# A long convolution split into even and odd positions: half-size transforms, sums and differences, columns dealt out anew

## Chip, cores and metric

One NeuronCore of one Trainium2 chip runs the whole program. The metric is device time of one execution in microseconds (us). TensorE is called PE, its weight loads PEld, VectorE DVE, ScalarE ACT, GpSimd POOL and SyncE SP.

## The reference

The program is three layers on 256 tokens of width 2048, batch 1, float32: a gated recurrent mixer, a forgetting-attention mixer, and a block with two branches and a feed-forward part. The change is in the first branch of that block, a Hyena mixer of width 1024:

```python
def two_sided_spectrum(h):
    kern = jnp.concatenate([h_fwd, jnp.zeros_like(h_fwd[:1]), h_bwd[:0:-1]], axis=0)
    return jnp.fft.rfft(kern, axis=0)

def long_conv(u, kf, bias):
    uf = jnp.fft.rfft(u, n=2 * L, axis=1)
    y = jnp.fft.irfft(uf * kf[None], n=2 * L, axis=1)[:, :L]
    return y + u * bias
...
    z = hx1 * long_conv(hv, kf[:, 0], hb[0])
    y_a = (hx2 * long_conv(z, kf[:, 1], hb[1])).astype(x.dtype)
...
    mixed = gate_a * (y_a @ w_branch_a[l]) + gate_b * (y_b @ w_branch_b[l])
```

L is 256. So there are two long convolutions one after the other over 1024 channels, each with its own filters, and then the product `y_a @ w_branch_a`. The product `y_b @ w_branch_b` of the other branch does not depend on them.

## The kernel before

**Matrix products.** Weights come as a stream of chunks of 512 KB (128x1024 floats) through a ring of four buffers. For each chunk ACT writes a rounded part `hi` and DVE the rest `lo` (`prep`, L539 and L1046; in loops `chunk`, L534 and L1040), and PE runs three passes for each tile (L1853 to L1855). SP starts the load of a ring slot as soon as `lo` of its old chunk is written. The product `y_b @ w_branch_b` (called br_b) is done in 16 *columns*, one chunk and 24 PE instructions each (`branch_column`): PE computes column f into PSUM bank f % 2, and DVE multiplies it by its gate (`filled`, L1738, counted in the semaphore `branch_b`). PE may not start column f before `branch_b` has reached f - 1. `ahead(f)` prepares the chunk that is four columns further on.

**The long convolution** is laid between those columns. It works in four *units* u: units 0 and 1 are the first and second convolution of channels 0 to 511, units 2 and 3 those of channels 512 to 1023, so unit 1 needs the output of unit 0 and unit 3 that of unit 2. Transforms are float32 matmuls with constant cosine and sine matrices (`dftm`, 256x256 each for forward and inverse). A float32 matmul is two instructions in the records (two passes). For each unit:

- `y_filters` (PE, L2280): the filters of 512 channels in time; `windowed` (DVE): times a window, then the sum (`y_SUM`) and the difference (`y_FB`) of forward and backward filter;
- `y_filter_cosines`, `y_filter_sines` (PE, L2267, 4 matmuls of 128x512 each): filter spectra, which ACT copies to `y_K` (L937);
- `y_turn` (PE, L2298, 8 transposes of 128x128), `turned` (ACT, L931): the input with positions on partitions (`y_U`);
- `y_input_spectrum` (PE, L2267 `y_T,dftm`): 4 cosine and 4 sine matmuls of 128x512 into banks 2, 3 and 6, 7;
- `spectra_product` (DVE, L1706 to L1713): six operations of 128x1024; in unit 3 twelve of 128x512;
- `y_back` (PE, L2337): 16 matmuls of 128x256, the inverse transform straight back to channels on partitions;
- `gated` (DVE, L1722 and L1729): adds the bias term and multiplies by the gate, which `y_turn` of the next unit waits for (`y_out`).

All orders are written out by hand, per engine. `columns_mid` and `columns_end` say which columns stand between the input spectrum and `y_back`, and which after it. After the last column comes `product(prod["br_a"])`, the product with `w_branch_a`; its input is the convolution's output, in pieces 2 and 3 (`branch_piece`: ACT rounds into `XH`, L518, DVE writes the rest into `XL`, L1111). `own_last` and `own_wait` make DVE wait for its own results.

Of the kernel before, what the change touches and what calls it, by code (L numbers as in the profile page):

```python
# [180 lines left out]
def program(nc, stream, h_in, params, consts, masks_a, mask_fox, mask_ml, dft, windows, z_pos, w1, w2, w3, out):  # L181
# [13 lines left out]
    with ExitStack() as ctx:  # L195
# [112 lines left out]
        with ExitStack() as ph:  # L308
# [9 lines left out]
            with ExitStack() as sub:  # L318
                w3_t = sb(sub, "w3_t", [FILT, 4, 512])
                y_win = sb(sub, "y_win", [P, 2, 2, 512])  # L320
                y_T = [sb(sub, f"y_T{s}", [P, 2, 512]) for s in range(2)]
                y_SUM = sb(sub, "y_SUM", [P, 2, 512])
                MR = sb(sub, "MR", [MH, 2, 4, SEQ])

            y_U = y_T[0]
# [186 lines left out]
        def _(act):  # L512
# [377 lines left out]
            def mixers():  # L890
# [38 lines left out]
                def turned(u):  # L929
                    act.wait_ge(S("y_ut"), u + 1)  # L930
                    act.activation(y_U[:, :, :], PS[:, 2:4, :], ACT.Copy).then_inc(S("y_u"), 1)  # L931
# [34 lines left out]
                ahead(columns_mid[3])  # L966
                act.wait_ge(S("y_out"), 4)
                branch_piece(3)
                ahead(columns_end[3])
# [47 lines left out]
        def _(dve):  # L1017
# [656 lines left out]
            def hyena():  # L1674
# [18 lines left out]
                def spectra_product(u):  # L1693
                    dve.wait_ge(S("y_uspec"), u + 1)
                    dve.wait_ge(S("y_k"), 2 * u + 2)
                    if u:
                        dve.wait_ge(S("y_inv"), u)

                    n_parts = 2 if u == 3 else 1
                    for part in range(n_parts):  # L1700
                        w = 512 // n_parts
                        cols = slice(w * part, w * part + w)
                        uc, us = PS[:, 2:4, cols], PS[:, 6:8, cols]
                        t0, t1 = (y_T[i][:, :, cols] for i in range(2))
                        k0, k1 = (y_K[:, i, :, cols] for i in range(2))
                        own_last(dve.tensor_tensor(t0, uc, k0, ALU.mult))  # L1706
                        own_last(dve.tensor_tensor(t1, us, k1, ALU.mult))
                        own_wait()
                        own(dve.tensor_tensor(t0, t0, t1, ALU.subtract), "y_spectrum", 2 * (u + part) + 1)
                        own_last(dve.tensor_tensor(t1, uc, k1, ALU.mult))  # L1710
                        own_last(dve.tensor_tensor(k0, us, k0, ALU.mult))
                        own_wait()
                        own(dve.tensor_tensor(t1, t1, k0, ALU.add), "y_spectrum", 2 * (u + part) + 2)  # L1713
                    dve.sem_inc(S("y_prod"), 1)

                def gated(u):

                    half, o = u // 2, u % 2
                    dve.wait_ge(S("y_inv"), u + 1)
                    for j in range(4):  # L1720
                        t = 4 * half + j
                        own_last(dve.scalar_tensor_tensor(out=HY[:, t, :], in0=HY[:, t, :],  # L1722
                                                          scalar=pc("hyena_bias", HT * o + t),
                                                          in1=PS[:, y_back_bank[u] + j // 2,
                                                                 SEQ * (j % 2):SEQ * (j % 2) + SEQ],
# [30 lines left out]
                columns((1,))  # L1756
                for u in range(4):
                    spectra_product(u)
                    if u == 3:
                        branch_piece(2)  # L1760
                    columns(columns_mid[u])
                    gated(u)
                    if u < 2:
                        windowed(u + 2)
                    if u == 3:
                        filled(14)
                        branch_piece(3)
                        ahead(14)
                        columns((15,))
                    else:  # L1770
                        columns(columns_end[u])
# [78 lines left out]
        def _(pe):  # L1850
# [420 lines left out]
            def y_filters(u):  # L2271
# [5 lines left out]
                for b in range(4):  # L2277
                    if u == 0 and b == 2:
                        pe.wait_ge(S("m_fw"), 2 * MH)
                    pe.matmul(PS[:, filter_bank[u][b], :], h2T[:, 128 * (b % 2):128 * (b % 2) + 128],  # L2280
# [11 lines left out]
            def y_turn(u):  # L2292
# [3 lines left out]
                for k in range(2):  # L2296
                    for j in range(4):
                        ins = pe.transpose(PS[:, 2 + k, 128 * j:128 * j + 128],  # L2298
                                           HY[:, 4 * (u // 2) + j, 128 * k:128 * k + 128], ident)
                ins.then_inc(S("y_ut"), 1)  # L2300

            def y_input_spectrum(u):
                pe.wait_ge(S("y_u"), u + 1)
                y_spectrum(2, cos_f, y_U)
# [4 lines left out]
                y_spectrum(6, sin_f, y_U).then_inc(S("y_uspec"), 1)  # L2309
# [16 lines left out]
            def y_back(u):  # L2326

                pe.wait_ge(S("y_spectrum"), 2 * u + 2)
                if u == 3:
                    pe.wait_ge(S("y_k"), 2 * u + 2)  # L2330
                for j in range(4):
                    if u == 3 and j == 2:
                        pe.wait_ge(S("y_spectrum"), 2 * u + 4)
                    n = 0
                    for part, m in enumerate((cos_i, sin_i)):
                        for f in range(2):
# [157 lines left out]
```

## Time and profile before

| | us |
|---|---|
| median of 3 runs | 2662.69 (2659.71 to 2662.83) |
| the profiled execution: its own time / its span | 2660.54 / 2658.5 |
| PE busy | 2609.9 (98%), 21346 instructions |
| DVE busy | 1567.9 (59%) |
| ACT busy | 1202.1 (45%) |
| mean granted PE clock | 0.996 |
| convolution phase (first filter spectrum to the start of br_a) | 1636.45 to 1787.87 |

The busy time of a group is the union of its instructions. A matmul's duration in the records is longer than the distance to the next, since matmuls overlap, so costs are read from start to start.

### The profile page before, as it was taken

To read this page: it belongs to the slowest core of one execution; us is meant where nothing else is said; L and a number is where in the kernel's file an instruction comes from. 1 tells how busy PE (TensorE), PEld (TensorE's weight loads), DVE (VectorE), ACT (ScalarE), POOL (GpSimd) and SP (SyncE) were. 2 spreads that over 40 slices of the span, in tenths; PEclk is the share of its full clock that TensorE was granted. 3 is DMA by queue.
4 is the path that set the end of the run, shared out by engine and by line. 5 is a ranking of instruction groups with operands and counts; after the bars stand their busy time and mean duration, and the time that the engine had idled before them with its cause. 6 is when DMAs were issued, how large, how long until landed. Compare 5 with 4: busy or idle time off the path is not lost.

```text
span 2658.5 us, 53149 instructions
## 1 busy us (share of the span) xinstructions
PE 2609.9 (98%) x21346; PEld 2537.8 (95%) x21346; DVE 1567.9 (59%) x1934; ACT 1202.1 (45%) x1404; POOL 44.2 (2%) x48
## 2 busy tenths in 40 slices
PE   8999999999999999999999999999999999999997
PEld 8999999999999999999999996679999999999997
DVE  6445777564465666677755456556565555554544
ACT  5344466543357655533435443124444444444442
POOL 0000121000000000000000000000000000000000
PEclk9999999999999999999999999999999999999999
DMA  6554532455544434555555553115555656565553
GB/s 225 175 178 163 171 104 76 167 174 183 174 174 153 139 114 149 193 196 190 192 193 185 193 194 104 48 65 193 188 193 185 202 184 200 188 198 192 189 198 128
DMA packets 123705, 446.05 MB, mean 168 GB/s; under 512 B 13594, under 2 KB 15925, under 8 KB 123440
## 3 DMA queue, kind: packets, MB, share of 16 engines
q1 hardware_dynamic: 122208, 438.82, 49.2%
q0 software_dynamic: 1360, 5.27, 0.6%
q8 instruction: 102, 1.67, 0.3%
q14 instruction: 35, 0.29, 0.0%
HBM read 441.94 MB, written 2.10 MB: 167 GB/s over the span
## 4 chain that ended last, share of the span: by engine, by line
PE 91%; DVE 4%; ACT 2%; issue 2%; DMA 0%; POOL 0%; DVEq 0%; SPq 0%; ACTq 0%
PE PS L1853 25%; PE PS L1855 25%; PE PS L1854 25%; PE PS L1916 2%; PE PS L1918 2%; PE PS L1917 2%; PE PS L2267 2%; PE PS L2337 1%; DVE lo L1046 1%; PE PS L2219 1%; ACT hi L539 0%; PE PS L2000 0%; PE PS L2016 0%; PE PS L2280 0%; PE PS L2099 0%
## 5 line engine op out<-in xcount | busy, mean ns | idle before, releaser
L1853 PE MATMUL PS<-XH,hi 128*128 128x256 f32 (+1 forms) x5152 | 1449.9, 281 | 21.6 <-DVE lo L1040 11.2
L1855 PE MATMUL PS<-XH,lo 128*128 128x256 f32 (+1 forms) x5152 | 1446.1, 281 | 0.0
L1854 PE MATMUL PS<-XL,hi 128*128 128x256 f32 (+1 forms) x5152 | 1441.5, 280 | 0.0
L1040 DVE TENSOR_TENSOR lo<-raw,hi 128x1024 fp32r<-128x1024 f32 x704 | 852.8, 1224 | 752.9 <-ACT hi L534 749.6
L534 ACT ACTIVATE hi<-raw 128x1024 fp32r<-128x1024 f32 x704 | 740.3, 1059 | 946.4 <-PE PS L1855 920.9
L1853 PEld LDWEIGHTS PS<-XH,hi 128*128 128x128 f32 x5152 | 970.7, 188 | 26.7 <-issue 18.8
L1854 PEld LDWEIGHTS PS<-XL,hi 128*128 128x128 f32 x5152 | 973.3, 189 | 1.4 <-issue 1.2
L1855 PEld LDWEIGHTS PS<-XH,lo 128*128 128x128 f32 x5152 | 970.6, 188 | 0.0
L1916 PE MATMUL PS<-XH,hi 128*128 128x256 f32 (+1 forms) x768 | 229.3, 299 | 0.3 <-DVE XL L1111 0.3
L1918 PE MATMUL PS<-XH,lo 128*128 128x256 f32 (+1 forms) x768 | 216.1, 281 | 0.0
L1917 PE MATMUL PS<-XL,hi 128*128 128x256 f32 (+1 forms) x768 | 215.9, 281 | 0.0
L1046 DVE TENSOR_TENSOR lo<-raw,hi 128x1024 fp32r<-128x1024 f32 x124 | 152.2, 1232 | 106.2 <-ACT hi L539 105.8
L1853 PE MATMUL PS<-GH,hi 128*128 128x256 f32 x704 | 194.4, 276 | 0.0
L1854 PE MATMUL PS<-GL,hi 128*128 128x256 f32 x704 | 194.4, 276 | 0.0
L1855 PE MATMUL PS<-GH,lo 128*128 128x256 f32 x704 | 194.4, 276 | 0.0
L539 ACT ACTIVATE hi<-raw 128x1024 fp32r<-128x1024 f32 x124 | 129.3, 1050 | 96.5 <-PE PS L1855 63.2
L1916 PEld LDWEIGHTS PS<-XH,hi 128*128 128x128 f32 x768 | 144.7, 188 | 2.9 <-issue 1.4
L1917 PEld LDWEIGHTS PS<-XL,hi 128*128 128x128 f32 x768 | 144.7, 188 | 1.5
L1918 PEld LDWEIGHTS PS<-XH,lo 128*128 128x128 f32 x768 | 144.4, 188 | 0.0
L1855 PEld LDWEIGHTS PS<-GH,lo 128*128 128x128 f32 x704 | 132.1, 188 | 0.0
L1854 PEld LDWEIGHTS PS<-GL,hi 128*128 128x128 f32 x704 | 132.1, 188 | 0.0
L1853 PEld LDWEIGHTS PS<-GH,hi 128*128 128x128 f32 x704 | 132.1, 188 | 0.0
(322 smaller groups left out, 1570.2 us busy)
## 6 DMA issues: line engine op xcount, KB each, us to landing
raw<-stream SPq DMA_DIRECT2D x828, 512.0 KB, 4.0
H<-h_in SPq DMA_DIRECT2D x4, 544.0 KB, 7.8
y_win<-windows POOLq DMA_DIRECT2D x2, 1024.0 KB, 7.2
out<-H SPq DMA_DIRECT2D x4, 512.0 KB, 3.8
w_t<-w POOLq DMA_DIRECT2D x2, 512.0 KB, 6.3
dftm<-dft POOLq DMA_DIRECT2D x1, 1024.0 KB, 8.0
ml_m<-mask_ml POOLq DMA_DIRECT2D x1, 512.0 KB, 3.9
a_m<-masks_a POOLq DMA_DIRECT2D x1, 272.0 KB, 6.0
```

The source lines that it names most:

```text
L534: act.activation(halves(hi, s, q.tokens), raw_halves(s), ACT.Copy).then_inc(hi_ready, 1)
L539: act.activation(halves(hi, k % RING, tokens_of(k)), raw_halves(k % RING), ACT.Copy).then_inc(hi_ready, 1)
L1040: dve.tensor_tensor(halves(lo, s, q.tokens), raw_halves(s), halves(hi, s, q.tokens).bitcast(F32), ALU.subtract)\
L1046: dve.tensor_tensor(halves(lo, k % RING, tokens_of(k)), raw_halves(k % RING), halves(hi, k % RING, tokens_of(k)).bitcast(F32), ALU.subtrac ...
L1853: pe.matmul(PS[:, bank, 0:n], w_hi, x_hi, start=start, stop=False)
L1854: pe.matmul(PS[:, bank, 0:n], w_hi, x_lo, start=False, stop=False)
L1855: return pe.matmul(PS[:, bank, 0:n], w_lo, x_hi, start=False, stop=stop)
L1916: pe.matmul(dst, hi[s][:, col], x_hi, start=k == 0, stop=False)
L1917: pe.matmul(dst, hi[s][:, col], x_lo, start=False, stop=False)
L1918: ins = pe.matmul(dst, lo[s][:, col], x_hi, start=False, stop=k == NT - 1)
L2219: ins = pe.matmul(PS[:, 4 + 2 * d + tb, 0:2 * P + 1], w[:, st, 128 * tb:128 * tb + 128], m_VT[:, st, h, :], start=st == 0, stop=st == 1)
L2267: ins = pe.matmul(PS[:, bank + f, :], dftm[:, m, k, 128 * f:128 * f + 128], src[:, k, :], start=k == 0, stop=k == 1)
```

## The change

What it does, in four parts:

1. **Order of positions and frequencies.** The constant matrices and windows are laid out anew: positions in the order even, then odd; frequencies k = 0 to 127, then 255 down to 128. For frequency k and its mirror 255 - k the even positions give the same cosine half and the odd ones the same but for its sign, so one 128x128 matrix serves for both. The filter matmuls and the transposes read their weights with a step of two (`h2T[:, b % 2::2]`, `HY[..., k::2]`).
2. **Input spectrum.** `y_parities` transforms the even and the odd half only (4 matmuls of 128x512 instead of 8). ACT copies the two odd halves from PSUM (`odds`), and DVE forms sum and difference (`butterflies`).
3. **Product and inverse.** `spectra_product` runs in two parts of 256 channels with eight operations each, the last two of which form sum and difference over the mirrored frequencies; `y_back` too has two parts, and each of its 16 matmuls moves 128 columns instead of 256. `gated` reads its PSUM operand with the two position halves interleaved.
4. **Columns.** One column goes between the two parts of `y_back`; column 1 moves from before unit 0 into it. PE no longer waits for `y_out` before br_a.

```diff
-            columns_mid = ((2, 3), (5, 6), (8, 9), (11, 12, 13))
-            columns_end = ((4,), (7,), (10,), (14, 15))
+            columns_mid = ((1, 2), (5, 6), (9, 10), (13, 14))
+            columns_last = (3, 7, 11, 15)
+            columns_end = ((4,), (8,), (12,), ())
...
+                def odds(u):
+                    for i in range(2):
+                        act.wait_ge(S("y_odd_spec"), 2 * u + i + 1)
+                        if i == 0:
+                            act.wait_ge(S("y_sums"), 2 * min(u + 2, 4))
+                        act.activation(y_FB[:, 1, i, :], PS[:, 3 + 4 * i, :], ACT.Copy).then_inc(S("y_odd"), 1)
...
-                ahead((0, 1))
+                ahead((0,))
                 for u in range(3):
+                    odds(u)
+                    ahead(columns_mid[u])
+                    ahead((columns_last[u],))
                     spectrum(u + 1, 0)
-                    ahead(columns_mid[u])
                     spectrum(u + 1, 1)
                     turned(u + 1)
                     ahead(columns_end[u])
+                odds(3)
...
+                def butterflies(u):
+
+                    if u:
+                        dve.wait_ge(S("y_inv"), 2 * u)
+                    for i in range(2):
+                        dve.wait_ge(S("y_uspec"), 2 * u + i + 1)
+                        dve.wait_ge(S("y_odd"), 2 * u + i + 1)
+                        even, odd = PS[:, 2 + 4 * i, :], y_FB[:, 1, i, :]
+                        own_last(dve.tensor_tensor(y_T[:, 1 - i, 0, :], even, odd, ALU.add))
+                        own_last(dve.tensor_tensor(y_T[:, 1 - i, 1, :], even, odd, ALU.subtract))
+                    own_wait()
+
+                def spectra_product(u, part):
+
                     dve.wait_ge(S("y_k"), 2 * u + 2)
...
+                    own_last(dve.tensor_tensor(acc, x0, k1, ALU.mult))
+                    own_last(dve.tensor_tensor(x0, x0, k0, ALU.mult))
+                    own_last(dve.tensor_tensor(k0, x1, k0, ALU.mult))
+                    own_last(dve.tensor_tensor(k1, x1, k1, ALU.mult))
+                    own_wait()
+                    own_last(dve.tensor_tensor(x1, k0, acc, ALU.subtract))
+                    own_last(dve.tensor_tensor(x0, x0, k1, ALU.add))
+                    own_wait()
+                    low, high = y_T[:, :, 0, cols], y_T[:, :, 1, cols]
+                    dve.tensor_tensor(acc, low, high, ALU.add).then_inc(S("y_spectrum"), 1)
+                    dve.tensor_tensor(low, low, high, ALU.subtract).then_inc(S("y_spectrum"), 1)
...
+                        y = HY[:, t, :].rearrange("p (n a) -> p n a", a=2)
+                        conv_out = PS[:, y_back_bank[u] + j // 2, SEQ * (j % 2):SEQ * (j % 2) + SEQ]
+                        own_last(dve.scalar_tensor_tensor(out=y, in0=y, scalar=pc("hyena_bias", HT * o + t),
+                                                          in1=conv_out.rearrange("p (a n) -> p n a", a=2),
                                                           op0=ALU.mult, op1=ALU.add))
...
+                for u in range(3):
+                    first, second = columns_mid[u]
+                    butterflies(u)
+                    spectra_product(u, 0)
+                    filled(first)
+                    spectra_product(u, 1)
+                    filled(second)
+                    filled(columns_last[u])
+                    ahead(first)
                     gated(u)
+                    ahead(second)
+                    ahead(columns_last[u])
                     if u < 2:
                         windowed(u + 2)
...
+                butterflies(3)
+                filled(13)
+                spectra_product(3, 0)
+                filled(14)
+                spectra_product(3, 1)
+                branch_piece(2)
+                ahead(13)
+                filled(15)
+                gated(3)
+                ahead(14)
+                branch_piece(3)
+                ahead(15)
...
+            def y_parities(bank, m):
+
+                pe.matmul(PS[:, bank + 1, :], dftm[:, m, 1, 0:128], y_U[:, 1, :], start=True, stop=True)\
+                    .then_inc(S("y_odd_spec"), 1)
+                return pe.matmul(PS[:, bank, :], dftm[:, m, 0, 0:128], y_U[:, 0, :], start=True, stop=True)
...
-                y_back(u)
+                y_back(u, 0)
+                branch_column(columns_last[u])
+                y_back(u, 1)
...
-            pe.wait_ge(S("y_out"), 4)
             pe.wait_ge(S("branch_b"), NT)
             product(prod["br_a"])
```

The input spectrum of unit 0 and the filter spectrum behind it, on PE. Before:

```order
L2267 MATMUL PS<-y_T,dftm 128x512 [waits y_u]
L2267 MATMUL PS<-y_T,dftm 128x512 x3
L2267 MATMUL PS<-y_T,dftm 128x512 [waits y_windowed]
L2267 MATMUL PS<-y_T,dftm 128x512 x3
L2267 MATMUL PS<-y_SUM,dftm 128x512 [waits y_sums]
L2267 MATMUL PS<-y_SUM,dftm 128x512 x3
```

The same place on PE in the changed kernel, where it now follows directly on `y_filters(1)`, without column 1 between:

```order
L2312 MATMUL PS<-w_t,h2T 128x512 x3
L2336 MATMUL PS<-y_T,dftm 128x512 [waits y_u]
L2338 MATMUL PS<-y_T,dftm 128x512
L2336 MATMUL PS<-y_T,dftm 128x512 [waits y_windowed]
L2338 MATMUL PS<-y_T,dftm 128x512
L2299 MATMUL PS<-y_SUM,dftm 128x512 [waits y_sums]
L2299 MATMUL PS<-y_SUM,dftm 128x512 x3
```

Eight matmuls of the input spectrum became four; those of the filter spectrum are as many as before.

The inverse transform of unit 0 on PE, before:

```order
L2337 MATMUL PS<-dftm,y_T 128x256 [waits y_spectrum]
L2337 MATMUL PS<-dftm,y_T 128x256 x15
L2267 MATMUL PS<-y_FB,dftm 128x512 [waits y_sums]
L2267 MATMUL PS<-y_FB,dftm 128x512 x3
L2298 MATMUL PS<-cst,HY 128x128 [waits y_out]
L2298 MATMUL PS<-cst,HY 128x128 x7
```

And its first part in the changed kernel, with the start of column 3 behind it:

```order
L2374 MATMUL PS<-dftm,y_FB 128x128 [waits y_spectrum]
L2374 MATMUL PS<-dftm,y_FB 128x128
L2374 MATMUL PS<-dftm,y_T 128x128 x2
L2374 MATMUL PS<-dftm,y_FB 128x128 x2
L2374 MATMUL PS<-dftm,y_T 128x128 x2
L1885 MATMUL PS<-XH,hi 128x256 [waits lo_ready,branch_b]
```

The moved operand shrinks from 256 to 128 columns, and the second eight matmuls stand behind a column (24 instructions).

The product of unit 3 on DVE, before: the second half of it, and what follows.

```order
L1706 TENSOR_TENSOR y_T<-PS,y_K 128x2x256 [waits y_spectrum]
L1707 TENSOR_TENSOR y_T<-PS,y_K 128x2x256
L1709 TENSOR_TENSOR y_T<-y_T 128x2x256 [waits dve_own]
L1710 TENSOR_TENSOR y_T<-PS,y_K 128x2x256 [waits y_spectrum]
L1711 TENSOR_TENSOR y_K<-PS,y_K 128x2x256
L1713 TENSOR_TENSOR y_T<-y_T,y_K 128x2x256 [waits dve_own]
L1111 TENSOR_TENSOR XL<-HY,XH 128x1024 [waits y_spectrum,xh_ready]
L1738 TENSOR_TENSOR MG<-MG,PS 128x256 [waits chunk_used]
```

In the changed kernel, behind the butterflies of unit 3: `filled(13)`, the product's part 0, `filled(14)` and the start of part 1.

```order
L1759 TENSOR_TENSOR MG<-MG,PS 128x256 [waits chunk_used,dve_own]
L1723 TENSOR_TENSOR y_FB<-y_T,y_K 128x2x256 [waits y_k]
L1724 TENSOR_TENSOR y_T<-y_T,y_K 128x2x256
L1725 TENSOR_TENSOR y_K<-y_T,y_K 128x2x256
L1726 TENSOR_TENSOR y_K<-y_T,y_K 128x2x256
L1728 TENSOR_TENSOR y_T<-y_K,y_FB 128x2x256 [waits dve_own]
L1729 TENSOR_TENSOR y_T<-y_T,y_K 128x2x256
L1732 TENSOR_TENSOR y_FB<-y_T 128x2x256 [waits dve_own]
L1733 TENSOR_TENSOR y_T<-y_T 128x2x256
L1759 TENSOR_TENSOR MG<-MG,PS 128x256 [waits chunk_used]
L1723 TENSOR_TENSOR y_FB<-y_T,y_K 128x2x256 [waits y_k]
```

Six operations for each half became eight, four butterflies came ahead of them, and the first of the `filled` now stands ahead of the product and not behind it.

## Rows read from the trace of the kernel before

**Rows 1.** The page's first part: busy time and share of the span.

```profile
PE 2609.9 (98%) x21346; PEld 2537.8 (95%) x21346; DVE 1567.9 (59%) x1934; ACT 1202.1 (45%) x1404; POOL 44.2 (2%) x48
```

**Rows 2.** Timeline of PE, unit 0 to 1: start, duration, line, operation, count.

```profile
1653.59 7.03 PE L2267 MATMUL PS<-y_T,dftm 128*128 128x512 f32 x16
1660.45 3.60 PE L2267 MATMUL PS<-y_SUM,dftm 128*128 128x512 f32 x8
...
1669.41 7.07 PE L2337 MATMUL PS<-dftm,y_T 128*128 128x256 f32 x32
1676.31 3.60 PE L2267 MATMUL PS<-y_FB,dftm 128*128 128x512 f32 x8
```

**Rows 3.** Timeline of PE, the transposes of unit 0 and what follows them.

```profile
1639.95 1.04 PE L2298 MATMUL PS<-cst,HY 128*128 128x128 f32 x8
1640.83 3.60 PE L2267 MATMUL PS<-y_FB,dftm 128*128 128x512 f32 x8
```

**Rows 4.** Groups by line: small float32 matmuls of another layer, summed busy, mean ns.

```profile
L2016 PE MATMUL PS<-AB,a_SS 128*128 128x64 f32 x128 | 17.8, 262 | 0.0
L2000 PE MATMUL PS<-a_VT,a_KT 128*128 128x128 f32 x128 | 16.9, 275 | 0.0
```

**Rows 5.** Waits of PE from 1625 to 1800: us in total, times, longest.

```profile
PE PS L1853 <- DVE MG L1738: 4.4, 1, 4.4
PE PS L1853 <- issue: 1.3, 1, 1.3
```

**Rows 6.** Timeline of DVE, product of unit 3 to column 11's gate.

```profile
1758.35 0.69 DVE L1706 TENSOR_TENSOR y_T<-PS,y_K 128x512 f32<-128x512 f32 x1 [4.49 <-PE PS L2267]
1758.95 0.68 DVE L1707 TENSOR_TENSOR y_T<-PS,y_K 128x512 f32<-128x512 f32 x1
1759.67 0.69 DVE L1709 TENSOR_TENSOR y_T<-y_T 128x512 f32<-128x512 f32 x1
...
1765.82 0.69 DVE L1713 TENSOR_TENSOR y_T<-y_T,y_K 128x512 f32<-128x512 f32 x1
1766.66 1.23 DVE L1111 TENSOR_TENSOR XL<-HY,XH 128x1024 fp32r<-128x1024 f32 x1
1767.80 0.41 DVE L1738 TENSOR_TENSOR MG<-MG,PS 128x256 f32<-128x256 f32 x1
```

**Rows 7.** Timeline of PE: end of column 12, start of 13, inverse of unit 3.

```profile
1763.55 0.28 PE L1855 MATMUL PS<-XH,lo 128*128 128x256 f32 x1
1768.27 0.58 PE L1853 MATMUL PS<-XH,hi 128*128 128x256 f32 x1 [4.44 <-DVE MG L1738]
...
1773.55 1.61 PE L2337 MATMUL PS<-dftm,y_T 128*128 128x256 f32 x5
```

**Rows 8.** Stretches: us, PE busy (count), PEclk (1.00 is full), DMA share, GB/s.

```profile
1763.50:1767.00 3.50, 0.33 (x3) 1.00 0.00 0
1767.00:1767.50 0.50, 0.00 (x0) 0.96 0.00 0
1767.50:1774.00 6.50, 5.73 (x26) 0.50 0.45 149
1774.50:1787.00 12.50, 12.02 (x79) 1.00 0.13 43
```

**Rows 9.** Timeline of DVE, `gated` of unit 0 (its first row with the wait).

```profile
1676.51 1.66 DVE L1722 SCALAR_TENSOR_TENSOR HY<-HY,par,PS 128x256 f32<-128x256 f32 x4 [3.75 <-PE PS L2337]
1678.20 1.22 DVE L1729 TENSOR_TENSOR HY<-HY 128x1024 f32<-128x1024 f32 x1
```

**Rows 10.** Groups of ACT: copies out of PSUM, and an operation of 128x512.

```profile
L937 ACT ACTIVATE y_K<-PS 128x1024 f32<-128x1024 f32 x8 | 8.2, 1029 | 70.8 <-DVEq L1714 39.5 <-PE PS L2267 31.3
L810 ACT ACTIVATE b_PT<-PS 128x384 f32<-128x384 f32 x16 | 7.8, 486 | 22.7 <-PE PS L2114 22.7
```

**Rows 11.** Waits of SP's queue from 1625 to 1800: what its weight loads waited for.

```profile
SPq L452 <- DVE lo L1046: 172.9, 16, 43.0
```

**Rows 12.** Timeline of DVE, the gate of column 15, the last `filled`.

```profile
1787.35 0.42 DVE L1738 TENSOR_TENSOR MG<-MG,PS 128x256 f32<-128x256 f32 x1
```

More of the change, by code:

```diff
@@ L966, in mixers @@
                 ahead(columns_mid[3])
+                ahead((columns_last[3],))
                 act.wait_ge(S("y_out"), 4)
                 branch_piece(3)
[L969 removed]
             q = prod["br_b"]
@@ L1691, in windowed @@
                         .then_inc(S("y_sums"), 1)
-                def spectra_product(u):
-                    dve.wait_ge(S("y_uspec"), u + 1)
-                    dve.wait_ge(S("y_k"), 2 * u + 2)
[L1696 to L1714, printed above, removed]
@@ new lines, in spectra_product @@
+                def spectra_product(u, part):
+                    dve.wait_ge(S("y_k"), 2 * u + 2)
+                    cols = slice(SEQ * part, SEQ * part + SEQ)
+                    acc = y_FB[:, 1, :, cols]
+                    x0, x1 = (y_T[:, i, :, cols] for i in range(2))
+                    k0, k1 = (y_K[:, i, :, cols] for i in range(2))
+                    own_last(dve.tensor_tensor(acc, x0, k1, ALU.mult))
[9 more added lines that the diff above has]
+                    dve.tensor_tensor(low, low, high, ALU.subtract).then_inc(S("y_spectrum"), 1)
+                    if part:
+                        dve.sem_inc(S("y_prod"), 1)
@@ L1755, in hyena @@
                 windowed(1)
[L1756 to L1761, printed above, removed]
+                for u in range(3):
[7 more added lines that the diff above has]
+                    ahead(first)
                     gated(u)
+                    ahead(second)
+                    ahead(columns_last[u])
                     if u < 2:
                         windowed(u + 2)
[L1765 to L1771, printed above, removed]
+                    columns(columns_end[u])
+                butterflies(3)
[10 more added lines that the diff above has]
+                ahead(15)
             q = prod["mg"]
@@ L2324, in branch_column, with y_back @@
                 ins.then_inc(chunk_used, 1)
-            def y_back(u):
-                pe.wait_ge(S("y_spectrum"), 2 * u + 2)
+            def y_back(u, part):
+                pe.wait_ge(S("y_spectrum"), 2 * (2 * u + part) + 2)
                 if u == 3:
                     pe.wait_ge(S("y_k"), 2 * u + 2)
[L2331 to L2336, printed above, removed]
-                            ins = pe.matmul(PS[:, y_back_bank[u] + j // 2, SEQ * (j % 2):SEQ * (j % 2) + SEQ],
-                                            y_T[part][:, f, 128 * j:128 * j + 128], dftm[:, m, f, :],
-                                            start=n == 0, stop=n == 3)
-                            n += 1
+                for j in (2 * part, 2 * part + 1):
+                    for a in range(2):
+                        col = SEQ * (j % 2) + 128 * a
+                        for i, m in enumerate((sin_i, cos_i)):
+                            w = (y_T[:, i, 0, :] if a else y_FB[:, 1, i, :])[:, 128 * j:128 * j + 128]
+                            ins = pe.matmul(PS[:, y_back_bank[u] + part, col:col + 128], w,
+                                            dftm[:, m, 0, 128 * a:128 * a + 128], start=i == 0, stop=i == 1)
                 ins.then_inc(S("y_inv"), 1)
```

30 lines of the change are left out of this document (14 added, 16 removed).

## The prediction

> **What bounds the kernel now.** First the busy shares: PE is busy for 98% of the span [rows 1], so time is won by taking work or idle time from PE, and what DVE or ACT do counts only where PE waits for them. Then the timeline of PE through one unit. From 1653.59 to 1660.45 stand the 16 passes of the input spectrum, 6.86 us or 0.429 a pass; the filter spectrum behind it has 8 passes, so it ends at 1660.45 + 3.43 = 1663.88; two columns follow up to 1669.41, 2.76 each; and the 32 passes of the inverse run to 1676.31, 6.90 or 0.216 a pass [rows 2]. Nothing lies between them: in units 0 to 2 PE is the bound. Third, the waits of PE in the phase: 4.4 us for a gate `filled`, once, and 1.3 once [rows 5]. The timeline puts the first into unit 3: PE ends column 12 soon after 1763.55 and starts column 13 at 1768.27 [rows 7], because DVE does the twelve operations of the product in one go from 1758.35, then the piece of `XL`, and only then the gate of column 11 at 1767.80 [rows 6]. The second is the start of br_a, which wants the gate of column 15; it begins at 1787.35 and ends at 1787.77 [rows 12]. Last, the granted clock. It stood at 1.00 up to 1767.0, fell to 0.50 before 1767.5, some 3.7 us after the last matmul, was 0.50 up to 1774 and 1.00 again behind that [rows 8]: the lower of the two levels, 1.2 GHz instead of 2.4.
>
> **Work taken from PE.** The input spectrum goes from 16 passes of 512 columns to 8: 8 x 0.429 = 3.43 us a unit, 13.7 in four. The inverse keeps its 32 passes but moves 128 columns in each. The nearest row is the transposes, also float32, 128x128, new weights each time: 8 from 1639.95 to 1640.83, 0.110 each [rows 3]. So 32 x 0.110 = 3.5 for 6.9, 3.4 a unit, 13.5 in four. From below 64 columns take no less than half of that, yet 128 such passes come to 17.8 us (0.139), and 128 passes of 128 columns to 16.9 (0.132), gaps between their groups counted in [rows 4]: weight loads, not columns, might set the pace. At 0.132 the inverse would save 2.8 less; I take 0.110, from a run without gaps as here, and see no reason for less. Together **27.2 us**.
>
> **The clock.** Column 13 took 1773.55 - 1768.27 = 5.28 instead of 2.76, and the passes of the inverse up to 1774 lost 0.3: **2.9 us**, if the new kernel does not let the clock fall.
>
> **Work added on DVE and ACT, and whether it hides.** The steps: operations of 512 elements start 0.60 apart, 0.72 where one waits for the one before [rows 6]; DVE sees a result of PE 0.20 after its last pass (1676.31, 1676.51) [rows 2, 9], PE one of DVE about 0.1 after its end. A product part is eight operations with two such waits: 3 x 0.60 + 0.72 + 0.60 + 0.72 + 0.60, then 0.69 for the last, 5.13 in all. A pair of butterflies is 0.60 + 0.72. ACT's copy of an odd half (128x512) lies between 0.49 and 1.03 [rows 10]; I take 0.6. Let T be the end of PE's input spectrum.
>
> *Units 1 and 2.* The second butterflies start at T + 0.24, part 0 at T + 1.6, and it is done at T + 6.7. PE needs it after a filter spectrum and two columns, T + 3.43 + 5.52 = T + 8.95. Part 1, behind one gate (0.34), ends at T + 12.2; PE wants it a half inverse and a column later, 8.95 + 1.76 + 2.76 = T + 13.5. Hidden, with 1.3 us of cover. The gated output: `y_inv` at T + 15.4, 1.66 + 1.24 us of work [rows 9] end at T + 18.3, and `y_turn` comes after the filter sines at T + 18.7. Hidden with 0.4.
>
> *Unit 0.* Here column 1 no longer stands between `y_filters(1)` and the input spectrum. DVE still does `windowed(1)`, whose last operation frees the buffer of the odd halves; ACT copies behind it, and the first butterflies start about 1 us after T instead of before it. Then part 0 just meets PE, and part 1 comes 0.9 late. **Lost: 0.9.**
>
> *Unit 3.* No filter spectrum gives cover. The gate of column 13 stands ahead of part 0 and waits for that column: T + 2.76 + 0.20. Part 0 starts 0.34 later at T + 3.3 and ends at T + 8.4; PE has ended column 14 at T + 5.5 and resumes at T + 8.5: 3.0 idle. Half inverse and column 15 last until T + 13.05; gate 14 and part 1 are done at T + 13.9: 0.9 idle. The inverse ends at T + 15.7; DVE does the piece of `XL`, a `lo` (1.15 each from start to start) and the gate of column 15, and br_a starts at T + 16.6: 0.9 idle. `XL` of piece 3, which br_a wants two chunks (5.5 us) later, is ready at about the same time. **Lost: 4.8** in the place of 4.44 + 1.34 = 5.8 before [rows 5].
>
> So idle time is 5.7 against 5.8: **0.1 us**. The strided weight reads touch 8 transposes a unit (and the filter matmuls, where the load lies under a pass of 512 columns). No row shows such a load; if it took twice as long it would cost 0.9 a unit, 2.5 in the phase, part of it absorbed. I take nothing, since the elements are no more. ACT is far from full, and the weight stream cannot hold PE back here: its queue waited 173 us for DVE's `lo` in this stretch [rows 11], and every later stage is the same work, started earlier.
>
> **The sum.** 27.2 + 2.9 + 0.1 = 30.2 off the profiled execution's own time, 2660.5: 2630.3. The median of the runs shown is 2.2 higher, the lowest run 0.8 lower; I lean a little to the median and say **2631**. Runs of one kernel scatter by about 0.1%, so 0.2% (5 us) is what can be told from no change.
>
> **A rule weighed.** The row shows `gated` with its four operations in 1.66 us when the PSUM operand is contiguous [rows 9]; the changed one reads it with the halves interleaved, a distance of 128 elements at each step, and no row has that. The Trainium skill ("SBUF — State Buffer", the note on cachelines) says that PSUM has lines of 8 bytes and that any non-contiguous pattern there significantly slows down matmuls. It speaks of matmuls, and this is DVE; by the row the sum stays 2631, by the rule carried over it would be the third case below.
>
> **The rivals.**
>
> 1. *The forecast*, 2631, own range 2627 to 2635: **0.62**.
> 2. *The clock falls in unit 3 again.* PE idles for 3.0 us there, then works 4.5 and idles 0.9. Before, the fall came 3.7 us after the last matmul [rows 7, 8]; that the idle now ends sooner speaks against it, that only 0.7 is missing, and that one fall in the trace fixes no limit, speaks for it. Price: 6.7 us at half clock as before, which doubles half an inverse (1.8) and adds 1.6 in column 15, less the 0.9 of waiting that goes: 2.5. Time 2633.5. **0.15.**
> 3. *DVE's reads slow down.* If the interleaved reads double `gated`, it takes 1.6 more, the cover of 0.4 is gone in three units (1.0 to 1.2 lost in each, some of it given back by shorter waits behind it), and two chunks after br_a starts the late piece 3 costs 0.9: about 2.8 in all, 2634. The same case holds operations of 512 elements at 0.70 apart instead of 0.60: twenty a unit make 2 us, which passes the 1.3 of cover and lengthens the stalls of units 0 and 3, near 5 us, 2636. Against it: the operations of unit 3 before have this very shape, 128x2x256, and stand 0.60 apart [rows 6]. **0.13.**
> 4. *Small passes don't pay.* Pace 0.132 and slow transposes as bounded above: 2.8 + 2.5, 2636. **0.06.**
> 5. *Slower: DVE becomes the bound.* The change gives DVE four butterflies and sixteen product operations a unit where it had six of double size. If each cost as much as one of 1024 elements (1.15 apart), the chain from T would end at T + 23 instead of T + 12.2, 9.5 behind PE in units 0 to 2 and 10 in unit 3: 38 more, 2669, slower by 8. It decides from about 1.05 us an operation. The rows have 0.60 [rows 6], so **0.02**.
> 6. *No change:* what is won comes back, since the weight stream or DVE's `lo` bounds the stages behind. The queue's waits speak against it [rows 11]: 2661, **0.02**.
>
> **Numbers.** The range 2626 to 2637 takes in cases 1 to 3 and most of 4, with the scatter of the runs. Cases 1 to 4 lie 24 to 35 us below, far beyond 0.2%: faster 0.96, same 0.02, slower 0.02.
>
> **What the new profile would show.** The input spectrum of a unit 3.43 us long; each half inverse 1.76, at 0.110 a pass; waits of PE for the product in unit 0 (0.9) and twice in unit 3 (3.0 and 0.9), one of 0.9 at br_a, none in units 1 and 2 but those for `y_K`; a granted clock of 1.00 throughout; and the phase from the first filter spectrum to br_a 121 us long instead of 151.4. The forecast is wrong if DVE's operations of 128x2x256 or the four of `gated` take longer than their rows, if passes of 128 columns are paced by their loads, or if the clock falls in unit 3.

## The result and the profile after

| | before | after |
|---|---|---|
| median, us | 2661.2 (4 runs) | 2632.86 (2630.43 to 2634.74, 4 runs) |
| ratio, 95% interval | | 0.9892 (0.988 to 0.9904) |
| span of the profiled execution | 2658.5 | 2631.7 |
| first filter spectrum to the start of br_a | 151.42 | 122.78 |

The change makes the kernel 28.3 us faster, 1.1%. A second series of the changed kernel (e5 below) gave 2634.76 against 2661.05, ratio 0.99 (0.9884 to 0.9917).

The first lines of the page of the changed kernel, busy times and span, answer to [rows 1]:

```profile
span 2631.7 us, 53153 instructions
PE 2584.1 (98%) x21314; PEld 2521.6 (96%) x21314; DVE 1587.5 (60%) x1984; ACT 1207.2 (46%) x1412; POOL 44.2 (2%) x48
```

PE is busy 25.8 us less, with 32 instructions fewer; DVE is busy 19.6 us more, and the span is 26.8 shorter. PE, busy for 98%, is still the bound of the whole.

The timeline of PE in unit 0 and unit 1 answers to [rows 2, 3]:

```profile
1654.36 1.12 PE L2336 MATMUL PS<-y_T,dftm 128*128 128x512 f32 x2
1655.32 1.02 PE L2338 MATMUL PS<-y_T,dftm 128*128 128x512 f32 x2
1656.18 1.02 PE L2336 MATMUL PS<-y_T,dftm 128*128 128x512 f32 x2
1657.04 1.02 PE L2338 MATMUL PS<-y_T,dftm 128*128 128x512 f32 x2
1657.90 3.60 PE L2299 MATMUL PS<-y_SUM,dftm 128*128 128x512 f32 x8
...
1702.20 0.60 PE L2374 MATMUL PS<-dftm,y_FB 128*128 128x128 f32 x4
...
1703.53 0.61 PE L2374 MATMUL PS<-dftm,y_T 128*128 128x128 f32 x4
1703.98 3.60 PE L2299 MATMUL PS<-y_FB,dftm 128*128 128x512 f32 x8
```

The input spectrum lasts from 1654.36 to 1657.90, 3.54 us instead of 6.86, and a half inverse from 1702.20 to 1703.98, 1.78, so 3.56 for a whole one instead of 6.90: 0.111 us a pass.

The waits of PE from 1625 to 1800 answer to [rows 5]:

```profile
PE PS L2374 <- DVE y_T L1733: 3.9, 3, 2.9
PE PS L1885 <- DVE MG L1759: 0.6, 1, 0.6
```

And their places in the timeline of PE:

```profile
1672.04 0.71 PE L2374 MATMUL PS<-dftm,y_FB 128*128 128x128 f32 x4 [0.40 <-DVE y_T L1733]
...
1753.08 0.71 PE L2374 MATMUL PS<-dftm,y_FB 128*128 128x128 f32 x4 [2.87 <-DVE y_T L1733]
...
1758.47 0.71 PE L2374 MATMUL PS<-dftm,y_FB 128*128 128x128 f32 x4 [0.58 <-DVE y_T L1733]
...
1761.07 0.39 PE L1885 MATMUL PS<-XH,hi 128*128 128x256 f32 x1 [0.55 <-DVE MG L1759]
```

One wait in unit 0, two in unit 3, one at br_a, and none for the product in units 1 and 2: the four places that the prediction named, 4.4 us in all where it had 5.7.

Stretches of PE in the changed kernel (us, PE busy, PEclk, DMA share, GB/s) answer to [rows 8]:

```profile
1639.00:1642.50 3.50, 3.50 (x5) 0.51 0.00 0
1642.75:1761.00 118.25, 113.48 (x659) 1.00 0.23 72
1424.25:1427.50 3.25, 3.25 (x18) 0.51 0.82 289
```

In unit 3 the clock stays at its upper level. But it stands at the lower one, 1.2 GHz, in two stretches where this did not happen in the profiled execution before, 1424 to 1427.5, ahead of the phase, and 1639 to 1642.5, in a filter spectrum that both kernels have. The same stretches before:

```profile
1424.25:1427.50 3.25, 3.25 (x31) 1.00 0.74 263
1636.50:1642.50 6.00, 6.00 (x20) 1.00 0.00 0
```

Each costs about half of 3.5 us. (A third such stretch, near 1018, stands in both profiles.) That closes the account: 28.6 us off the phase and 1.8 given back ahead of it make the 26.8 of the spans; behind the phase both kernels take 870.6.

### The profile page after: what moved, and what is told of

It is laid out like the page before. It is cut to its first block, busy times and chain, and to the rows that moved or that the text cites. A ratio compares the mean times of both kernels' runs of the same rounds, so it can differ in the third digit from the quotient of the medians.

```text
span 2631.7 us, 53153 instructions
## 1 busy us (share of the span) xinstructions
PE 2584.1 (98%) x21314; PEld 2521.6 (96%) x21314; DVE 1587.5 (60%) x1984; ACT 1207.2 (46%) x1412; POOL 44.2 (2%) x48
## 4 chain that ended last, share of the span: by engine, by line
PE 90%; DVE 5%; ACT 3%; issue 1%; DMA 0%; POOL 0%; DVEq 0%; SPq 0%; ACTq 0%
PE PS L1885 25%; PE PS L1887 25%; PE PS L1886 25%; PE PS L1948 2%; PE PS L1949 2%; PE PS L1950 2%; PE PS L2299 1%; DVE lo L1057 1%; ACT hi L540 1%; PE PS L2251 1%; PE PS L2032 0%; PE PS L2048 0%; PE PS L2131 0%; PE PS L2108 0%; PE PS L2022 0%
## 5 line engine op out<-in xcount | busy, mean ns | idle before, releaser
L1885 PE MATMUL PS<-XH,hi 128*128 128x256 f32 (+1 forms) x5152 | 1449.4, 281 | 16.7 <-DVE lo L1051 11.6
```

The source lines that it names most:

```text
L1885: pe.matmul(PS[:, bank, 0:n], w_hi, x_hi, start=start, stop=False)
```

## The experiments

Phase means the time from the first filter spectrum to the start of br_a in the profiled execution, 122.78 us in the changed kernel. Times of e1 to e6 are medians, those of e7 to e12 one execution each; the kernel before ran at 2662.66 beside e1 to e4, at 2661.05 beside e5 to e8 and at 2660.59, once, beside e9 to e12. "Over the changed kernel" is counted from its 2632.86, taken beside a base of 2661.2. Since the base moves by 1.5 us between these series, a difference of medians across them is no finer than that, and the phase is the sharper number.

**e1, the inverse with 256 columns.**

```diff
-                            ins = pe.matmul(PS[:, y_back_bank[u] + part, col:col + 128], w,
-                                            dftm[:, m, 0, 128 * a:128 * a + 128], start=i == 0, stop=i == 1)
+                            ins = pe.matmul(PS[:, y_back_bank[u] + part, SEQ * (j % 2):SEQ * (j % 2) + SEQ], w,
+                                            dftm[:, m, 0, :], start=i == 0, stop=i == 1)
```

> The changed kernel, but each matmul of the inverse moves 256 columns again (its output is overwritten by the next, so the result is not the convolution). Theory: the inverse's passes are paced by their columns, 0.216 against 0.110 us, so PE gets 4 x 3.4 = 13.5 us more; the longer first half gives DVE more time, which takes the stalls of 0.4 to 0.6 us ahead of each second half away and the wait at br_a, some 1.5 to 2 us in all. Expected 11 to 12.5 us over the changed kernel, about 2644 to 2645. Rival (small passes are paced by weight loads, or the gain is elsewhere): under 8 us.

Measured: 2644.43 us, ratio 0.9931 (0.9915 to 0.9948), 11.6 over the changed kernel, phase 136.65, 13.9 more. In the profile the timeline of PE has

```profile
1671.21 1.02 PE L2374 MATMUL PS<-dftm,y_FB 128*128 128x256 f32 x4
...
1674.66 3.60 PE L2299 MATMUL PS<-y_FB,dftm 128*128 128x512 f32 x8
...
1760.48 2.08 PE L2374 MATMUL PS<-dftm,y_FB 128*128 128x256 f32 x4 [2.88 <-DVE y_T L1733]
...
1766.81 0.47 PE L1885 MATMUL PS<-XH,hi 128*128 128x256 f32 x1
```

A half inverse takes 3.45 us instead of 1.78, 13.4 for eight, and of the waits only the first of unit 3 is left, which gives 1.5 back: 11.9. The phase has 13.9, since here the clock fell in unit 3; its first half inverse took 6.33 us instead of 3.45, 2.9 of which the clock cost. Without it the phase is 11.0 longer, at the lower edge of what was expected and well above the rival's 8. The 0.9 between 11.0 and 11.9 is PE's own. Around a wait its work takes longer from start to start: the second half inverse of unit 3, between two waits, takes 2.05 us in the changed kernel and not 1.78. Where the waits go in e1, this goes too. The columns set the pace of these passes: 0.216 us at 256, 0.111 at 128.

**e2, the input spectrum twice.**

```diff
+                pe.matmul(PS[:, bank + 1, :], dftm[:, m, 1, 0:128], y_U[:, 1, :], start=True, stop=True)
                 pe.matmul(PS[:, bank + 1, :], dftm[:, m, 1, 0:128], y_U[:, 1, :], start=True, stop=True)\
                     .then_inc(S("y_odd_spec"), 1)
+                pe.matmul(PS[:, bank, :], dftm[:, m, 0, 0:128], y_U[:, 0, :], start=True, stop=True)
                 return pe.matmul(PS[:, bank, :], dftm[:, m, 0, 0:128], y_U[:, 0, :], start=True, stop=True)
```

> The changed kernel, with each matmul of the input spectrum done twice, as many as before the change. The result is unchanged. Theory: 8 passes of 0.429 more in each unit, 13.7 us, less about 0.9 in unit 0, where DVE's late start is covered by them: 12.8 us over the changed kernel, about 2646; the stall of 2.9 in unit 3 stays, since it is counted from the end of the spectrum. Rival (DVE or the weight stream sets the phase): clearly less than 10.

Measured: 2645.67 us, ratio 0.9939 (0.9923 to 0.9956), 12.8 over the changed kernel; phase 1636.66 to 1772.44, 13.0 longer. Unit 3 keeps its waits:

```profile
1764.44 0.71 PE L2376 MATMUL PS<-dftm,y_FB 128*128 128x128 f32 x4 [2.88 <-DVE y_T L1733]
...
1772.44 0.38 PE L1885 MATMUL PS<-XH,hi 128*128 128x256 f32 x1 [0.55 <-DVE MG L1759]
```

In unit 3 as expected: DVE's chain hangs on the end of the input spectrum, so PE work ahead of it shifts everything by its own length. In unit 0 the wait for the product is gone, as expected too; it had been 0.40 us, not the 0.9 that the expectation takes off.

**e3, the new transforms with the old columns.**

```diff
-            columns_mid = ((1, 2), (5, 6), (9, 10), (13, 14))
-            columns_last = (3, 7, 11, 15)
-            columns_end = ((4,), (8,), (12,), ())
+            columns_mid = ((2, 3), (5, 6), (8, 9), (11, 12, 13))
+            columns_end = ((4,), (7,), (10,), (14, 15))
...
                 y_back(u, 0)
-                branch_column(columns_last[u])
                 y_back(u, 1)
...
+                    butterflies(u)
+                    spectra_product(u, 0)
+                    spectra_product(u, 1)
+                    if u == 3:
+                        branch_piece(2)
+                    columns(columns_mid[u])
+                    gated(u)
```

> The new transforms alone: half-size input spectrum, butterflies and half-size inverse, but the columns dealt as before the change, both halves of the inverse together, DVE doing both product parts ahead of any gate. Theory: PE's work is that of the changed kernel, but DVE's 20 operations stand in the way: second half of the inverse 1.2 late in units 0 to 2, the transposes 0.6 late in each, and in unit 3 column 13 is 7.8 late, for which the clock falls as before: 8 us of idle time and about 3 of clock over the changed kernel, about 2644. If the columns did not matter: 2633.

Measured: 2642.48 us, ratio 0.9924 (0.9907 to 0.994), 9.6 over the changed kernel; phase 1636.86 to 1770.76 = 133.90, 11.1 longer. The waits of PE in the phase:

```profile
PE PS L1874 <- DVE MG L1757: 7.6, 1, 7.6
PE PS L2363 <- DVE y_T L1731: 2.8, 3, 0.9
PE PS L1874 <- issue: 1.3, 1, 1.3
PE PS L2319 <- DVE HY L1748: 0.8, 3, 0.3
```

And the stretch of PE around column 13 in e3:

```profile
1750.25:1760.25 10.00, 5.53 (x26) 0.50 0.30 83
```

12.5 us of waits instead of 4.4, 8.1 more, and column 13 at half clock again, 1754.72 to 1760.00, 5.28 instead of 2.76; with the start of the inverse about 2.9. The waits came out a little under the expected ones in units 0 to 2 (0.9 and 0.3 where 1.2 and 0.6 were said), and 7.6 where 7.8 was said in unit 3. Of the 28 us that the change wins, the transforms with the old columns win 20 (2662.66 - 2642.48), and the new order on top of them the rest. The rest holds also what the dropped wait for `y_out` ahead of br_a is worth, which e3 puts back and which was not tried by itself.

**e4, the kernel before with one gate moved.**

```diff
                     for part in range(n_parts):
+                        if part:
+                            filled(11)
...
                     if u == 3:
                         branch_piece(2)
-                    columns(columns_mid[u])
+                        ahead(11)
+                        columns((12, 13))
+                    else:
+                        columns(columns_mid[u])
```

> The kernel before the change, with one step moved: DVE does the gate of column 11 between the two halves of unit 3's product and not behind them. Theory: the idle 4.44 us ahead of column 13 goes, and with it the stretch at half clock (2.9), nothing else moves: 7.3 us under the kernel before, about 2654. Granted clock 1.00 throughout the phase. Rival (the clock falls for another reason than the idle time): 4.4 under, 2657, and the clock still falls.

Measured: 2656.17 us, ratio 0.9976 (0.9967 to 0.9986), 6.5 under the kernel before; phase 1636.41 to 1780.35, 7.5 shorter. The waits of PE in the phase:

```profile
PE PS L2272 <- DVE y_SUM L1686: 1.5, 1, 1.5
PE PS L1858 <- issue: 1.4, 1, 1.4
```

And the stretch of PE over the whole phase in e4, at full clock:

```profile
1636.50:1780.00 143.50, 141.91 (x696) 1.00 0.20 63
```

The wait of 4.44 and the half clock go together, as the forecast had it (4.4 + 2.9 = 7.3). It is the profile that says so: the interval of the ratio, 3.7 to 8.8 us, holds the rival's 4.4 as well. So 6.5 of the 28 us could be had in the old kernel with its old transforms, by moving one gate.

**Columns alone.** The new deal of the columns on the old arithmetic was not tried, since it would race: the first half of the inverse writes PSUM bank 2 while DVE still reads the input spectrum there for part 1. In the new arithmetic the butterflies move the spectrum out of PSUM first. So in units 0 to 2 the column between the halves is something that the new arithmetic makes possible.

**e5, the changed kernel again.**

> The changed kernel once more, as the base for the next run. 2633 as before. Its profile tells whether the granted clock falls in unit 3: of the kernels with an idle stretch of 2.87 to 2.88 us there, the changed one and the one with eight spectrum matmuls showed no fall, the one with 256 columns did. If the idle time alone decided, it would be the same in every execution; if not, it may fall here.

Measured: 2634.76 us (2632.27 to 2635.7); phase 1638.69 to 1761.47, 122.78 as before, no fall in unit 3, and one in the filter spectrum at 1639 again.

**e6, two steps of DVE moved in unit 3.**

```diff
-                filled(13)
                 spectra_product(3, 0)
-                filled(14)
+                filled(13)
                 spectra_product(3, 1)
+                filled(14)
                 branch_piece(2)
-                ahead(13)
                 filled(15)
+                ahead(13)
                 gated(3)
```

> The changed kernel with two steps of DVE moved in unit 3: the gate of column 13 behind part 0 of the product and not ahead of it, the gate of column 15 ahead of the chunk's lo and not behind it. Theory: the idle time ahead of the first half inverse goes from 2.9 to 1.3, that at the start of br_a from 0.55 to 0, and 0.8 comes up two chunks later, where piece 3 of XL is late: 1.7 us less in all, about 2631. Rival: DVE's total is the bound of unit 3 and the idle time only moves: no gain, 2633.

Measured: 2632.39 us (2628.09 to 2633.81), ratio to the kernel before 0.9889 (0.9872 to 0.9905), 2.4 under e5, less than the runs of either scatter. The profile can tell it:

```profile
1751.59 0.71 PE L2374 MATMUL PS<-dftm,y_FB 128*128 128x128 f32 x4 [1.10 <-DVE y_T L1733]
...
1756.99 0.71 PE L2374 MATMUL PS<-dftm,y_FB 128*128 128x128 f32 x4 [0.61 <-DVE y_T L1733]
...
1765.24 0.36 PE L1885 MATMUL PS<-XH,hi 128*128 128x256 f32 x1 [0.53 <-DVE XL L1122]
```

The first wait of unit 3 is 1.10 instead of 2.87, that at br_a is gone, and 0.53 comes up two chunks later: 1.8 us less idle time from the inverse on, as expected. The total in the runs leaves it open.

**e7 and e8, a longer idle stretch in unit 3.** Operations of `butterflies(3)` are done again behind `filled(13)`: `extra_pair(1)` in e7, `extra_pair(0)` and `extra_pair(1)` in e8.

```diff
+                def extra_pair(i):
+                    even, odd = PS[:, 2 + 4 * i, :], y_FB[:, 1, i, :]
+                    own_last(dve.tensor_tensor(y_T[:, 1 - i, 0, :], even, odd, ALU.add))
+                    own_last(dve.tensor_tensor(y_T[:, 1 - i, 1, :], even, odd, ALU.subtract))
```

> The changed kernel with two more DVE operations of 512 elements (two of the butterflies of unit 3 done again) ahead of part 0 of unit 3's product; the result is unchanged. Idle time there 2.9 + 1.3 = 4.2 us, about that of the kernel before (4.44). If a longer idle stretch makes the clock fall, it is at half speed behind it for some 3.5 to 7 us, which costs 2 to 3 us on top of the 1.3.

> The same with four such operations: idle time 2.9 + 2.5 = 5.4 us. The clock falls, 2 to 3 us on top of the 2.5.

Measured, one execution each: 2634.22 and 2636.59 us. Stretches of PE around the idle time in e7:

```profile
1749.50:1753.75 4.25, 0.21 (x2) 1.00 0.00 0
1754.00:1757.25 3.25, 3.25 (x16) 0.50 0.00 0
1757.50:1762.00 4.50, 4.50 (x42) 1.00 0.00 0
```

And one in e8:

```profile
1752.75:1759.50 6.75, 5.86 (x27) 0.50 0.00 0
```

PE idles 4.20 and 5.40 us, and the clock falls in both, for 3.5 us in e7, which is just the half inverse at half speed (1753.91 to 1757.31, 3.40 instead of 1.80), and for 7 in e8, where it reaches the column behind (3.99 instead of 3.01). But little of this shows in the time: the waits of 0.58 and 0.55 behind it are gone in both. The phase is 124.09 in e7 (1637.82 to 1761.91), 1.3 over the changed kernel, which is the added idle time and nothing more, and 126.41 in e8 (1636.35 to 1762.76), 3.6 over, 1.1 more than the added idle time. The expected 2 to 3 us on top did not come in either.

**e9 to e12, is it the strided filters?** The fall at 1639 stood in every profile of the changed arithmetic so far and in none of the old one. One thing differs there: the filter matmuls load `h2T` with a step of two. So e9 and e10, one kernel twice, are the changed kernel with contiguous loads in unit 0, and e11 and e12 the kernel before with the step of two there. In all four unit 0 convolves with its filter's positions in another order than its tables want, so the result is not the convolution.

```diff
# e9, e10, on the changed kernel
-h2T[:, b % 2::2]
+h2T[:, b % 2::2] if u > 0 else h2T[:, 128 * (b % 2):128 * (b % 2) + 128]
# e11, e12, on the kernel before
-h2T[:, 128 * (b % 2):128 * (b % 2) + 128]
+h2T[:, b % 2::2] if u == 0 else h2T[:, 128 * (b % 2):128 * (b % 2) + 128]
```

> The changed kernel, where the four filter matmuls of unit 0 (only those) read their weights contiguous and not with a step of two, so the filters of unit 0 are in the wrong order of positions. In all eight profiles of kernels with the step the clock fell in the filter spectrum that follows, for about 3.5 us, and in both profiles without it it did not. If the strided loads ahead of the 1.54 us wait are the reason: no fall at 1636 to 1643, phase 1.7 us shorter, about 121.1. If it is chance: a fall here or in the next run.

> The same kernel once more: by the strided loads no fall at 1636 to 1643 in either of the two, by chance one or both.

> The kernel before the change, with a step of two in the weights of the four filter matmuls of unit 0 (their result is in the wrong order of positions). By the strided loads: the clock falls in the filter spectrum behind them, phase 1.7 us longer than 151.42. By chance: as before, no fall, or one of the two.

> The same kernel once more: by the strided loads a fall in both.

Measured: 2633.72, 2632.17, 2662.43 and 2660.22 us. The stretch with the first filter spectrum, in e9:

```profile
1636.00:1644.00 8.00, 7.20 (x19) 0.79 0.00 0
```

In e10:

```profile
1636.00:1644.00 8.00, 7.36 (x19) 0.79 0.00 0
```

In e11:

```profile
1636.00:1644.00 8.00, 6.45 (x21) 0.79 0.00 0
```

In e12:

```profile
1636.00:1644.00 8.00, 7.39 (x24) 1.00 0.00 0
```

A mean of 0.79 over 8 us is half clock for 3.4 of them: the clock fell in e9 and e10 without the strided loads, and did not fall in e12 with them. The theory falls. e11 and e12 are one kernel and differ in this, so the fall varies between executions. That does not make it even chance in both kernels: over all profiles it came in ten of ten with the new arithmetic and in one of four with the old. Whether something else in the changed kernel brings it on stays open. The same holds in unit 3. The stretch there in e9:

```profile
1752.75:1756.25 3.50, 3.50 (x32) 1.00 0.00 0
```

And in e10, the same kernel:

```profile
1752.75:1756.25 3.50, 3.50 (x19) 0.51 0.00 0
```

Both idle 2.87 us ahead of it. What this fall costs can be read from the starts behind it, the second half inverse and br_a. In e9:

```profile
1756.96 0.71 PE L2375 MATMUL PS<-dftm,y_FB 128*128 128x128 f32 x4 [0.61 <-DVE y_T L1733]
...
1759.56 0.38 PE L1885 MATMUL PS<-XH,hi 128*128 128x256 f32 x1 [0.55 <-DVE MG L1759]
```

And in e10:

```profile
1757.69 0.61 PE L2375 MATMUL PS<-dftm,y_FB 128*128 128x128 f32 x4
...
1759.43 0.38 PE L1885 MATMUL PS<-XH,hi 128*128 128x256 f32 x1
```

PE's work up to the second half is 1.5 us longer in e10, but both waits are gone and the second half is 0.3 shorter, and the phase is 122.79 us (1636.64 to 1759.43) against 122.76 in e9 (1636.80 to 1759.56). DVE's chain sets the time here, and a fall of 3.5 us fits into what PE would have waited. The phases of e11 and e12 are 151.76 and 151.23, where the kernel before has 151.42: e11 pays 1.7 for the fall at 1637, but stands at the lower level for only 3.5 us in unit 3 and not for 7.

## Why the prediction was right, point by point

- **Input spectrum, 3.43 a unit.** Right: 3.54 in unit 0, 3.43 in unit 1 (1685.19 to 1688.62); e2 puts it back and finds 12.8.
- **Inverse, 0.110 a pass.** Right: 0.111. Passes of 128 columns behind one another keep the pace of the transposes [rows 3]. The prediction set the 0.132 and 0.139 of [rows 4] aside because of gaps between groups, and that reading was wrong: busy time holds no gaps, but it counts the last pass of each short run to its end. Four passes of 64 columns that start at 332.13 count 0.56 us, though the next instruction starts at 332.52. The choice of 0.110 was right all the same. e1 puts the columns back.
- **The clock, 2.9.** Right as the price of the fall before: e4 takes the wait away and finds 7.5 for both. "A granted clock of 1.00 throughout" was wrong: it stood at 1.2 GHz for 3.5 us in the first filter spectrum. In unit 3 it did stay up in the profiled execution, but the reason for trusting in that was too simple, and there was luck in it. The forecast said that the idle time "now ends sooner" than the 3.7 us after which the clock had fallen. In e1 the same idle stretch of 2.88 us did bring a fall, some 2 us after the last matmul (idle from 1757.60, lower level before 1759.75). Over all profiles with this idle stretch it fell in two of six, so the second rival's chance, 0.15, looks low. Its price of 2.5 us was wrong too: in e10 the fall costs nothing in the phase, because the waits behind it, 1.2 us in e9, are gone. The rival knew of this, but took off only 0.9, and its 7 us at half clock came out at 3.5.
- **DVE hides in units 1 and 2.** Right: no wait for the product there. The 20 operations run at 0.60 to 0.72 apart, as read from [rows 6].
- **Unit 0, 0.9 lost.** It was 0.40. The mechanism is there: DVE idles 0.79 for ACT's copy and begins the butterflies 1.0 behind T (1657.90):

```profile
1658.91 0.69 DVE L1712 TENSOR_TENSOR y_T<-PS,y_FB 128x512 f32<-128x512 f32 x1 [0.79 <-ACT y_FB L939]
```

  The size was off by half a microsecond. Half of it is PE, whose first half inverse and column 3 took 4.78 and not 4.52; the other half is DVE, whose part 1 let PE go on at T + 14.1 where the prediction has T + 14.4.
- **Unit 3 and br_a, 3.0 + 0.9 + 0.9.** Measured 2.87 + 0.58 + 0.55. Each late step behind the first is less late, since PE's own part between them took longer than summed: 4.81 and not 4.52 for the half inverse and column 15, 2.05 and not 1.76 for the second half.
- **`gated` with interleaved reads.** The four operations take what they took, 1.66 us as in [rows 9]:

```profile
1704.18 1.66 DVE L1745 SCALAR_TENSOR_TENSOR HY<-HY,par,PS 128x256 f32<-128x256 f32 x4 [0.23 <-PE PS L2374]
```

  The sentence of the Trainium skill ("SBUF — State Buffer", the note on cachelines) on non-contiguous patterns in PSUM speaks of matmuls and does not carry over to this DVE operation.
- **The strided weight loads, nothing.** They were put at nothing "since the elements are no more", and that was not quite right. The load takes longer, and each set of eight transposes 0.07 to 0.08 us more than before, 0.3 in the phase (last section).
- **DVE as the bound, and no change.** Both fell, with 0.60 an operation and a phase 28.6 shorter. e3 shows how near the first is: with DVE's work in one piece PE waits 12.5 us. And in unit 3 DVE is the bound, as e9 and e10 show.
- **The sum.** 2631 against 2632.9. The phase came to 122.8 where 121 was said, and the difference is the fall of the clock at 1639, 1.7 us, which the prediction did not have. The profiled execution, 2633.55, is 3.3 over its 2630.3, and the two falls at 1424 and 1639 make 3.5. Without them two errors remain that cancel: the waits are 1.3 us shorter than forecast, and PE's own work around them is longer by about as much. That is not all luck, since where DVE's chain sets the time, what PE spends on its own it does not wait. In unit 0 half of the smaller wait is DVE's earlier end, and that part is luck.

## What to carry over

Halving a transform by parity moves work from PE to DVE. It paid here because PE had no gaps and DVE's new chain fits under work that PE has anyway. So count the chain from the end of the matmuls it hangs on, and deal the independent work so that some lies between two halves of the consumer. Look at the order alone first: one gate moved in the old kernel wins 6.5 us (e4), almost a quarter of the whole change. At the end of such a phase, where the cover runs out, a gate that PE wants soon must not stand behind a long product, nor one that waits for PE ahead of it (e6, 1.8 us less idle time, not told apart in the total). What PE loses in a wait can be more than the wait, since the clock may fall with it (e4). It need not be: where PE would wait again for a slower chain, the fall is taken up there (e9 against e10).

## What the hardware showed unexpectedly

**The clock can fall after short waits, and not in every execution.** The filter spectrum at the start of the phase waits 1.5 us for `y_SUM` in all kernels. The clock fell there for about 3.5 us (cost 1.7) in 11 of 14 profiled executions, all but those of the kernel before, e4 and e12. Those with the new arithmetic are ten, and it fell in all ten; of the four with the old it fell in one (e11). Ahead of the phase, near 1424, it fell behind a wait of 1.8 us in all but that of the kernel before, and near 1018, behind one of 1.2, in six of 14 (before, changed, e5, e6, e7 and e11). In unit 3 it goes with the length of the idle stretch, but not with it alone: none with 1.10 us (e6), two of six with 2.87 or 2.88 (e1 and e10, not the changed kernel, e2, e5 and e9), all six with 4.20 (e7), 4.43 (e12), 4.44 (before, e11), 5.40 (e8) and 7.62 (e3). It stayed low for about 3.5 us in e7, e10 and e11, about 7 in e1, e8, e12 and before, and about 10 in e3. Such falls can account for part of the scatter between executions: the four runs of the changed kernel show mean granted clocks of 0.996 (2633.55 and 2634.74) and 0.998 (2632.16 and 2630.43). The step of the weight loads is not the reason (e9 to e12). What decides whether a short wait brings a fall, and for how long, stays open.

**A weight load with a step of two is slower, and nearly hidden.** The loads of the transposes before the change, with minimum, median and maximum in ns:

```profile
L2298 PEld LDWEIGHTS PS<-cst,HY x32: 138/140/142, 1639.5 to 1748.3; 128*128 128x128 f32 x32
```

And after it:

```profile
L2330 PEld LDWEIGHTS PS<-cst,HY x32: 194/209/209, 1643.1 to 1738.1; 128*128 128x128 f32 x32
```

140 ns have become 209. The eight transposes of unit 3, which follow on work at full clock and have a column behind them in both kernels, before:

```profile
1747.65 1.04 PE L2298 MATMUL PS<-cst,HY 128*128 128x128 f32 x8
1748.44 0.36 PE L1853 MATMUL PS<-XH,hi 128*128 128x256 f32 x1
```

And after:

```profile
1737.41 1.11 PE L2330 MATMUL PS<-cst,HY 128*128 128x128 f32 x8
1738.27 0.36 PE L1885 MATMUL PS<-XH,hi 128*128 128x256 f32 x1
```

From start to start 0.79 us became 0.86, 0.07 more, about what one of the eight loads takes longer; the other units show 0.07 to 0.08 as well (in unit 0, 0.88 and 0.95). So seven of the eight longer loads cost nothing, it seems; that it is the first that shows was not tried.
